# Sharing the last stage of a decoder step among VectorE, ScalarE and GpSimd

## The reference

```
x = x + _hier_moe(h2, ...)      # each row: two of 32 experts, weighted by gates g0 and g1
y = _rms_norm(x, final_norm_g)  # x * rsqrt(mean(x*x) + eps) * g
```

## Time and profile before

| what | value |
|---|---|
| runs of the kernel | 1448.42, 1444.77, 1443.24 us; median 1444.77 us |
| profiled execution | 1446.99 us, its span 1445.2 us |
| engine busy over the span | PE 89%, DVE 45%, POOL 32%, ACT 28% |
| last stage, first load issued to the end of the span | 1403.56 to 1445.2 us |
| DVE in the last stage | 27 instructions, 1406.44 to 1440.57 us |

### The profile page before, as it was taken

One profiled execution on the slowest core, in us unless ns is written; L12 is line 12 of the kernel. 1 busy time (PEld: TensorE's weight loads), 2 busy tenths in 40 slices (PEclk: granted clock), 3 DMA queues, 4 the chain that ended last, 5 costly groups with the idle time before them and its releaser, 6 DMA issues. The chain is left out here.

```text
span 1445.2 us, 32259 instructions
## 1 busy us (share of the span) xinstructions
PE 1280.4 (89%) x13766; PEld 983.7 (68%) x13766; DVE 650.6 (45%) x1339; ACT 409.2 (28%) x856; POOL 469.2 (32%) x398
## 2 busy tenths in 40 slices
PE   7988899999999999999999999878754999998960
PEld 6777689889878978988987977767643333333320
DVE  2759763455245246245434624635434322222228
ACT  2243134234224213423432522431110122221214
POOL 1616272363254336237225425434001111111100
PEclk9999899999999999999999999988866999999985
DMA  9788527735834843863682463471056998999968
GB/s 276 251 217 247 159 94 240 239 104 192 277 105 135 273 152 107 260 206 104 206 279 89 153 215 116 136 124 29 20 208 266 354 361 359 417 417 416 409 248 320
DMA packets 217735, 317.28 MB, mean 220 GB/s; under 512 B 15332, under 2 KB 187952, under 8 KB 209000
## 3 DMA queue, kind: packets, MB, share of 16 engines
q1 hardware_dynamic: 205176, 277.51, 57.2%
q10 hardware_dynamic: 5792, 20.78, 4.1%
q0 software_dynamic: 6624, 16.92, 3.0%
HBM read 295.45 MB, written 27.01 MB: 223 GB/s over the span
## 5 line engine op out<-in xcount | busy, mean ns | idle before, releaser
L1533 PE MATMUL psum<-arena 128*128 128x256 f32 (+3 forms) x1536 | 311.2, 357 | 2.5 <-issue 2.5
L1533 PEld LDWEIGHTS psum<-arena 128*128 128x128 f32 x1536 | 257.3, 194 | 33.0 <-issue 3.1
L2381 PE MATMUL psum<-arena 128*64 128x512 f32 (+1 forms) x832 | 167.8, 608 | 7.4 <-DMA arena<-in_exp_w 7.4
L1236 DVE COPY_PREDICATED arena<-arena,psum 128x128 f32<-128x128 int32 x280 | 85.2, 304 | 141.8 <-PE psum L1722 134.9
L1529 PE MATMUL psum<-arena 128*128 128x128 f32 x1152 | 138.6, 280 | 3.6 <-DVE arena L1102 3.6
L669 POOL TENSOR_TENSOR arena<-arena 128x768 f32<-128x768 f32 (+1 forms) x32 | 59.1, 1847 | 244.0 <-ACT arena L900 244.0
L1529 PEld LDWEIGHTS psum<-arena 128*128 128x128 f32 x1152 | 134.0, 195 | 6.2 <-issue 5.8
L2381 PEld LDWEIGHTS psum<-arena 128*64 128x64 f32 (+1 forms) x832 | 51.9, 134 | 106.3 <-issue 104.1
L1491 PE MATMUL psum<-arena 64*64 64x64 f32 x3264 | 118.1, 224 | 4.1 <-issue 1.2
L1491 PEld LDWEIGHTS psum<-arena 64*64 64x64 f32 x3264 | 106.1, 138 | 21.7 <-issue 13.9
L1801 PE MATMUL psum<-arena 128*128 128x256 f32 x512 | 117.5, 389 | 0.8 <-ACT arena L977 0.8
(11 more groups left out here) (399 smaller groups left out, 1955.1 us busy)
## 6 DMA issues: line engine op xcount, KB each, us to landing
arena<-in_w_in SPq DMA_DIRECT2D x96, 1024.0 KB, 6.2
arena<-in_exp_w SPq DMA_DIRECT2D x96, 1024.0 KB, 16.8
arena<-in_w_out SPq DMA_DIRECT2D x32, 1024.0 KB, 5.8
arena<-in_w_in SPq DMA_DIRECT2D x24, 512.0 KB, 5.2
arena<-y_d SPq DMA_DIRECT2D x16, 512.0 KB, 10.9
arena<-in_x_prompt ACTq DMA_DIRECT2D x15, 512.0 KB, 5.7
arena<-in_w_in SPq DMA_DIRECT2D x8, 576.0 KB, 5.1
arena<-in_w_in SPq DMA_DIRECT2D x8, 560.0 KB, 4.1
```

The source lines that it names most:

```text
L1236: ins = v.copy_predicated(h3(att_b)[:, h:h + 2, :], b3(q_mask[4 * half + j], 2, 64), new)
L1533: ins = mm(b[:, 0:n], hT[:, c, :], w[:, c, 0:n], start=(c == 0), stop=(c == KC - 1))
L2381: ins = mm(bank[2 + q % 2][at:at + width, :].rearrange("p (m n) -> p m n", m=2), xT[q % 2][:, c, at:at + width], w13[n % NB][:, :, c, :], ...
```

## The change

DVE no longer touches the sample rows, and they move from the first place of `sequence` to the fourth. GpSimd sums them with four `tensor_tensor` (multiply, add, multiply, add), each of 8 partitions by 1024 columns; its gate operands are single values read again for each column. For three positions, `POOLED` = 2, 3 and 5 (tile 2, the sample rows, tile 4), the norm is split in two: ACT multiplies `tot` by rstd (an ACTIVATE of type Copy, raising `f_scaled`), then GpSimd multiplies by `fg` in place (raising `f_weighed`), and SP issues the store, behind its loads in the program. ACT waits for the earlier store of the same `fo` buffer before it scales. DVE's `half` has one buffer in place of two. The other six positions keep DVE's norm and ACT's store. The order in which SP loads is unchanged: sample, then tiles 0 to 7.

```diff
--- before.py
+++ after.py
@@ -2524,7 +2524,50 @@
         out_s = O[1].rearrange("b s d -> (b s) d")
         rows = [slice(t * P, t * P + P) for t in range(NT)] + [slice(NT * P, NT * P + NS)]
         count = [P] * NT + [NS]
-        sequence = [NT] + list(range(NT))
+        sequence = [0, 1, 2, NT] + list(range(3, NT))
+        AT_S = sequence.index(NT)
+        POOLED = (2, AT_S, 5)
+
+        def n_pooled(n):
+
+            return sum(m < n for m in POOLED)
+
+        def n_scaled(n):
+
+            return n - n_pooled(n)
+
+        def n_summed(n):
+
+            return n if n <= AT_S else n - 1
+
+        @block.gpsimd
+        def _(pool):
+            g = nc.gpsimd
+
+            def weigh(n):
+                t = sequence[n]
+                u, R = n % 3, slice(0, count[t])
+                pool.wait_ge(step("f_scaled"), n_pooled(n) + 1)
+                g.tensor_tensor(fo[u][R, :], fo[u][R, :], fg[R, :], ALU.mult).then_inc(step("f_weighed"), 1)
+
+            def sample_sums():
+                R, u = slice(0, NS), AT_S % 3
+                by = [gate[R, 2 * NT + k:2 * NT + k + 1].to_broadcast([NS, D]) for k in range(2)]
+                pool.wait_ge(step(f"x2_in{NT}"), 16)
+                pool.wait_ge(step(f"y2_in{NT}_0"), 16)
+                g.tensor_tensor(X[1][R, :], y2[NT][R, 0:D], by[0], ALU.mult).then_inc(step("f_sample"), 1)
+                pool.wait_ge(step("f_sample"), 1)
+                g.tensor_tensor(X[1][R, :], X[1][R, :], x2[NT][R, :], ALU.add).then_inc(step("f_sample"), 1)
+                pool.wait_ge(step(f"y2_in{NT}_1"), 16)
+                g.tensor_tensor(Y[1][R, :], y2[NT][R, D:2 * D], by[1], ALU.mult).then_inc(step("f_sample"), 1)
+                pool.wait_ge(step("f_sample"), 3)
+                pool.wait_ge(step("f_out"), n_scaled(AT_S - 3) + 1)
+                g.tensor_tensor(tot[u][R, :], X[1][R, :], Y[1][R, :], ALU.add).then_inc(step("f_sample"), 1)
+
+            pool.wait_ge(step("fg_in"), 16)
+            sample_sums()
+            for n in POOLED:
+                weigh(n)
 
         @block.sync
         def _(sp):
@@ -2535,8 +2578,12 @@
 
             sp.wait_ge(step("y_all"), 1)
             sp.dma_start(x2[NT][0:NS, :], x2_d[rows[NT], :]).then_inc(step(f"x2_in{NT}"), 16)
-            for t in sequence:
+            for t in [NT] + list(range(NT)):
                 load_y(t)
+            for n in POOLED:
+                t = sequence[n]
+                sp.wait_ge(step("f_weighed"), n_pooled(n) + 1)
+                sp.dma_start(out[rows[t], :] if t < NT else out_s, fo[n % 3][0:count[t], :]).then_inc(step(f"f_stored{n % 3}"), 16)
 
         @block.scalar
         def _(act):
@@ -2544,19 +2591,27 @@
 
             def store(n):
                 t = sequence[n]
-                act.wait_ge(step("f_out"), n + 1)
+                act.wait_ge(step("f_out"), n_scaled(n) + 1)
                 act.dma_start(out[rows[t], :] if t < NT else out_s, fo[n % 3][0:count[t], :]).then_inc(step(f"f_stored{n % 3}"), 16)
 
             for n, t in enumerate(sequence):
                 u, R = n % 3, slice(0, count[t])
                 st = fs[R, 4 * n:4 * n + 4]
-                act.wait_ge(step("f_sum"), n + 1)
+                if n == AT_S:
+                    act.wait_ge(step("f_sample"), 4)
+                else:
+                    act.wait_ge(step("f_sum"), n_summed(n) + 1)
                 a(Y[0][R, :], tot[u][R, :], ACT.Square, accum_out=st[:, 0:1]).then_inc(step("f_rs"), 1)
                 act.wait_ge(step("f_rs"), 3 * n + 1)
                 a(st[:, 1:2], st[:, 0:1], ACT.Ln, scale=1.0 / D, bias=eps[R, :]).then_inc(step("f_rs"), 1)
                 act.wait_ge(step("f_rs"), 3 * n + 2)
                 a(st[:, 2:3], st[:, 1:2], ACT.Exp, scale=-0.5).then_inc(step("f_rs"), 1)
-                if n:
+                if n in POOLED:
+                    act.wait_ge(step("f_rs"), 3 * n + 3)
+                    if n >= 3:
+                        act.wait_ge(step(f"f_stored{u}"), 16 * (n // 3))
+                    a(fo[u][R, :], tot[u][R, :], ACT.Copy, scale=st[:, 2:3]).then_inc(step("f_scaled"), 1)
+                if n and n - 1 not in POOLED:
                     store(n - 1)
             store(NTT - 1)
             for u in range(3):
@@ -2571,14 +2626,16 @@
                 u, R = n % 3, slice(0, count[t])
                 dve.wait_ge(step(f"x2_in{t}"), 16)
                 dve.wait_ge(step(f"y2_in{t}_0"), 16)
-                if n >= 2:
-                    dve.wait_ge(step("f_sum"), n - 1)
-                half = X[n % 2]
+                if n_summed(n):
+                    dve.wait_ge(step("f_sum"), n_summed(n))
+                half = X[0]
                 v.scalar_tensor_tensor(half[R, :], y2[t][R, 0:D], gate[R, 2 * t:2 * t + 1], x2[t][R, :],
                                        ALU.mult, ALU.add).then_inc(step("f_half"), 1)
-                dve.wait_ge(step("f_half"), n + 1)
-                if n >= 3:
-                    dve.wait_ge(step("f_out"), n - 2)
+                dve.wait_ge(step("f_half"), n_summed(n) + 1)
+                if n - 3 in POOLED:
+                    dve.wait_ge(step("f_scaled"), n_pooled(n - 3) + 1)
+                elif n >= 3:
+                    dve.wait_ge(step("f_out"), n_scaled(n - 3) + 1)
                 dve.wait_ge(step(f"y2_in{t}_1"), 16)
                 v.scalar_tensor_tensor(tot[u][R, :], y2[t][R, D:2 * D], gate[R, 2 * t + 1:2 * t + 2], half[R, :],
                                        ALU.mult, ALU.add).then_inc(step("f_sum"), 1)
@@ -2594,8 +2651,9 @@
 
             dve.wait_ge(step("fg_in"), 16)
             for n in range(NTT):
-                sums(n)
-                if n:
+                if n != AT_S:
+                    sums(n)
+                if n and n - 1 not in POOLED:
                     normed(n - 1)
             normed(NTT - 1)
```

## The result

The changed kernel takes 1453.51 us (median of 17 runs, 1450.28 to 1457.84) against 1446.49 us of the kernel before in the same comparison (17 runs, 1443.24 to 1452.96). The ratio is 1.0048, with a 95% interval of 1.0035 to 1.0061: slower, by 6.9 us (5.1 to 8.8), with the prediction's line of 0.5% inside the interval.

The account below looks back on a forecast made before the run. DVE was taken to bound the last stage; 11.7 us of turns against 3.5 us of gain made 8.2 us more, 1444.77 + 8.2 = 1453.0 us. The range was 1445.0 to 1455.5, the forecast's own 1450.5 to 1455.5.

Parts of the forecast that it names:

- the prediction's line of 0.5%: Whole kernel: a measurement can tell about 0.5%, 7.2 us, from no change; the line for slower is at 1452.0 us.
- What bounds the stage: Last stage: DVE sets the end, busy 24.05 of 24.30 us, with the loads close behind it.
- What the order takes off: DVE in the last stage: 22 of 27 instructions stay, ending 3.5 us sooner if the added work costs DVE nothing.
- GpSimd's lengths: GpSimd's seven last-stage instructions: 1.90 us with a repeated input, 2.36 us with streamed ones, no discount for eight partitions.
- The turns: Last stage: DVE instructions with two SBUF inputs and GpSimd's take turns, costing 11.7 us; full price had chance 0.77.
- The sample's three turns: First addition at tile 0's first sum 1.8 us, second multiplication between its sums 1.6, last addition at tile 2's sums 2.07.
- The queue rival: No turns; SP's store of position 2 queues behind loads, delaying ACT's scaling of position 5: 1.6 us later, 1446.4 us; chance 0.10.
- The rival beside it: Last stage: no turns, and the store lands in 6.6 us: 1.5 us sooner, 1443.3 us; chance 0.07.
- The size: Whole kernel: 8.2 us more, added to the median 1444.77 to give 1453.0 us.
- My chance of 0.62: Whole kernel: chance that the result lies above 1452.0 us, four fifths of the case of turns at full price.
- Neither overtakes twice: DVE and GpSimd in the convolution stage's trace: they take turns, and neither goes ahead of the other twice.

Follow-up runs that it names:

- e1: Changed kernel with GpSimd's seven last-stage instructions made fills that read no SBUF, sample's sums and three positions' weights left out: stage 43.6 us, ratio 1.0015.
- e2: Changed kernel with `half` and a copy of the norm's weights in PSUM, so only first sums have two SBUF inputs: stage 43.2 us, ratio 1.0009.
- e5: e1 with the stores of positions 2, 3 and 5 on ACT's queue, none on SP's behind the loads: stage 41.9 us.
- e8: Changed kernel with one more GpSimd multiplication, 8 partitions by 1024 columns, behind each of the three weightings: stage 54.6 us, ratio 1.0087.
- e7: e2 with six output buffers, and ACT multiplying y_a by its gate into PSUM for positions 0, 1, 5, 7: stage 42.1 us, ratio 1.0002.

## Why the prediction was right, point by point

- **What bounds the stage.** DVE, with loads behind it: as forecast. The DMA engines' share fell to 0.36 in the last 14 us while DVE was still busy.
- **What the order takes off.** I had 3.5 us; it is 3.0, worked out as 10.8 us of turns less the 7.8 by which DVE's last end moved (from 37.0 to 44.8 us after the stage's start). A first sum right behind another tile's second sum starts 1.42 us later (1423.75 to 1425.17), not 1.30, and the order has three such places: 0.4 of the missing 0.5 us.
- **GpSimd's lengths.** 1.90 and 2.36 us forecast, 1.88 and 2.33 measured, and eight rows got no discount.
- **The turns.** Forecast 11.7 us. By the six long sums less 1.28 each: 1.64 + 1.51 + 1.96 + 1.87 + 1.96 + 1.87 = 10.8 us. The last four, each with an instruction of two streamed inputs, cost 1.87 to 1.96 us, where the forecast had 2.07. The sample's three turns stand where the forecast put them, and each weighting met a sum as forecast, though about 1 us sooner (the first began 22.5 us after the stage's start, not 23.4). e1 and e2 show that the reads make them.
- **The queue rival.** It was right as a mechanism and absent from the result, since the turns gave the store time to land: issued at 1427.27, it landed 4.1 us later, and ACT began the scaling that needs its buffer at 1433.38. Without turns (e1) the stage is 1.9 us longer than before; the forecast for that case was 1.6. The rival beside it, no turns and a store that lands in 6.6 us, was priced too low: it had 1.5 us less than before, and e5, the nearest run, has 0.3 more. Its sum left out DVE's own wait for the store of position 1, 2.9 us there.
- **The size.** 8.2 us forecast, 7.9 in the stage, 6.9 (5.1 to 8.8) in the timed runs. 1453.0 was forecast and 1453.51 measured, but part of that nearness is luck: the median of before moved from 1444.77 to 1446.49 with more runs, and 8.2 us on top of that would be 1454.7. In the stage, too, two errors offset each other: the turns came out 0.9 us below their sum, and the gain 0.5 below its own. My chance of 0.62 for a loss over 0.5% was high for an effect that lies on that line.
- **"Neither overtakes twice"** was too strong, as e8 shows; the sum didn't need it.

## What to carry to other kernels

An idle GpSimd is no free second VectorE: before moving elementwise work to it from a stage that DVE bounds, count the DVE instructions with two SBUF inputs that will run at that time, and charge each GpSimd instruction that reads SBUF most of its length (here 1.5 to 2.0 us for lengths of 1.88 and 2.33). In the profile look for lengths, not for waits, as a blocked instruction is shown as busy (3.24 us for 1.28). Where one operand of a DVE instruction lay in PSUM, its turns went away (e2, and all of them in e7), and then the next limit showed: here the stores, whose landing frees the buffers, and ACT.

## What the runs showed of the hardware that was not expected

A reading GpSimd instruction doesn't block all of DVE: a second sum with one SBUF and one PSUM input kept 1.281 us at most, beside GpSimd's at 2.35. This was expected. The Trainium skill (SBUF — State Buffer, "Who interferes with whom") states that a VectorE instruction with at most one SBUF input, outside the modes in which it uses both of its port pairs, does not contend with GpSimd. It also states that one with two SBUF inputs contends with a GpSimd instruction that reads SBUF and not with one that only writes it. e2 agrees with the first, at 1.281 us, and e1 with the second, at 1.28 us.

What was not expected is the order in e8, where a waiting DVE sum let two GpSimd instructions pass and was recorded at 5.20 us.
